# Attention groups reordered to B, C, A with paired scores and half-bank turns, and the in-projection's weight subtractions moved from DVE to GpSimd

## The chip, the core and the metric

The kernel runs on one core of a Trainium2 chip. The metric is the device time of one execution in microseconds. TensorE (PE) multiplies matrices from SBUF into PSUM, which has four double banks here (`ps[0]` to `ps[3]`, each 128 partitions by 1024 float32, that is two banks of 512). DVE (VectorE) and ACT (ScalarE) read PSUM and SBUF, POOL (GpSimd) reads SBUF only, SP issues most DMAs.

## The reference

Two layers over 1024 tokens of width 1024, all float32. In each layer a normed input goes through one projection of 2820 columns, which three groups of heads share, each with its own attention. Their outputs are concatenated (1024 wide), projected and added; then comes an MLP of width 4096.

```python
h = rmsnorm(x, g_mix[l]);  proj = h @ w_in[l]
aq, ak, av, bq, bk, bv, cq, ck, cv, cf = jnp.split(proj, offsets, axis=-1)
# A: 4 heads x 2 maps of dim 64, chunk-causal, alibi:  a = softmax(s0) - lam * softmax(s1);  o = rmsnorm(a @ v) * (1 - lam_init), v is 128 wide
# B: 4 query heads on 2 key heads, keys of the last 128 tokens (two blocks), alibi, a sink in the softmax's sum
# C: 4 heads, causal, forget gate:  s + cum[q] - cum[k],  cum = cumsum(log_sigmoid(cf + c_fbias))
x = x + jnp.concatenate([o_a, o_b, o_c], axis=-1) @ w_out[l]
x = x + jnp.square(jax.nn.relu(rmsnorm(x, g_mlp[l]) @ w_up[l])) @ w_down[l]
# after both layers: rmsnorm(x, g_final)
```

## The kernel before

**Precision.** Every product of float32 operands is made of three fp32r matmuls: high by high, high by low, low by high. The high part is a rounding copy by ACT, the low part a subtraction by DVE. This holds for weights, activations, queries, keys, values and probabilities.

**Dense work.** All matrices are kept transposed, features in partitions, tokens along the free side. A slab is 128 output columns of a weight matrix: 1024x128, loaded into `w_raw` by two DMAs, split into `w_hi` and `w_lo` (two slots). A slab's product with the activations is eight chunks of 128 contraction rows; one chunk is six matmuls of 512 columns (`piece`, L1192 to L1199, and `products`, L1136 to L1151). A layer has 23 slabs of in-projection, 8 of out-projection and 64 of MLP.

**Attention.** Eight pairs of maps per layer: four of A (a head's two maps), two of C and two of B (two heads each). For each pair there are eight blocks of 128 queries; block i sees i+1 blocks of keys (in B at most two). In A and B one step is one query block with both maps, in C one step is one query block of one head, so a C pair has sixteen steps. PE makes scores in `ps[0]` (L1259 to L1269), DVE adds the bias and takes the row maximum (`biased_max`, L933), ACT exponentiates (L629). For A, DVE combines both maps (`combine`, L952). PE transposes the probabilities block by block into `ps[2]` (`turn_probs`, L1271), ACT and DVE split them into `pt_hi` and `pt_lo` (L597 and L922, four blocks at a time), PE multiplies by the values into `ps[3]` (`values`, L1283), DVE adds the two halves of the result (`sum_values`).

**Scores.** In A and C the scores of one map fill up to both banks of `ps[0]`, so a map's scores wait until DVE has read those of the map before. A map's operands lie in 64 partitions (0 to 63 or 64 to 127). In B a map needs one bank, and the two maps' scores are issued one behind the other, in different banks.

**Order.** It is written out by hand and every engine walks the same list of steps (`Run`, L105). In step t PE issues: scores of t, a chunk of the in-projection, values of t-2, scores of t's second map (A), another chunk, transposes of t-1, the remaining chunks (L1346 to L1380). The in-projection's chunks are spread over the steps by `PIECES` and `END_PIECES` (L99 and L100): a pair's steps carry the three slabs of the next pair. The order is A (a loop over two pairs, twice), C, then C, B, B. Only the first four slabs are computed ahead of attention. The last slab is done near the start of B: the last pair of B carries no chunk.

**Around it.** C's bias is cum[q] - cum[k] plus the causal mask, written to `probs` by ACT (L594) and DVE (L1003). The attention outputs of all heads are transposed after the last step (`turn_out`, L1391) and split by ACT and DVE; then the out-projection runs. The layer's input `xt` (4 MB) is saved to DRAM by one DMA on SP's queue once `h` is complete (L395), in front of the load of slab 2, and comes back in two DMAs. DVE computes `w_lo` for all slabs (L809, L841); POOL only adds squares and scales A's outputs.

## Time and profile before

| | us |
|---|---|
| median of 3 runs (lowest, highest) | 2849.33 (2838.36, 2854.39) |
| the profiled execution's own time | 2837.89 |
| its span, first to last instruction | 2835.8 |
| TensorE busy | 2723.2 (96%) |
| DVE busy | 1226.4 (43%) |
| ACT busy | 958.7 (34%) |
| POOL busy | 92.5 (3%) |
| mean granted TensorE clock | 0.965 |

A busy share is taken over the whole span. Matmuls overlap in the records, since they are pipelined: the distance between two starts is what a matmul costs, not the duration of one. The granted clock is in parts of 2.4 GHz: 1.0 is 2.4 GHz and 0.5 is 1.2 GHz, and a value in between is a mixture over the stretch.

### The profile page before, as it was taken

What the parts mean: (1) busy time and instruction counts of PE and PEld (TensorE: products, weight loads), DVE (VectorE), ACT (ScalarE), POOL (GpSimd) and SP (SyncE); (2) the same over time, 40 slices, a digit from 0 to 9 for tenths busy, and PEclk for the clock granted to TensorE, in tenths of its full rate; (3) what the DMA queues carried; (4) which work ended last, traced back from release to release, by engine and by line L of the source; (5) the groups of instructions that cost most, each with busy time, mean ns of one, the idle gap of its engine ahead of it and who ended that gap; (6) DMA issues with size and microseconds to landing.
All of it is one profiled execution on the core that took longest, in us unless ns stands there. A gap on an engine that the chain in (4) does not pass through costs nothing.

```text
span 2835.8 us, 35362 instructions
## 1 busy us (share of the span) xinstructions
PE 2723.2 (96%) x12809; PEld 2211.0 (78%) x12809; DVE 1226.4 (43%) x2444; ACT 958.7 (34%) x1700; POOL 92.5 (3%) x51
## 2 busy tenths in 40 slices
PE   7999999979999999999999999998899999999998
PEld 6777777768888888888877777776788888888887
DVE  5565665654322322223436666656443223232334
ACT  4444454552321212112234444545423122130223
POOL 0000010001000000000200001000020000000001
PEclk9999999959999999999999999998899999999998
DMA  4100000012111111111130000000211111111112
GB/s 153 38 23 23 22 23 16 8 38 82 45 52 45 47 50 49 47 50 46 44 104 23 23 22 23 16 23 8 82 52 45 45 51 48 48 44 52 44 52 74
DMA packets 214389, 126.25 MB, mean 45 GB/s; under 512 B 14702, under 2 KB 213400, under 8 KB 213528
## 3 DMA queue, kind: packets, MB, share of 16 engines
q1 hardware_dynamic: 211176, 121.95, 14.4%
q10 hardware_dynamic: 3120, 3.15, 0.3%
q8 instruction: 48, 0.79, 0.1%
q14 instruction: 45, 0.37, 0.0%
HBM read 112.49 MB, written 12.58 MB: 44 GB/s over the span
## 4 chain that ended last, share of the span: by engine, by line
PE 84%; DVE 6%; ACT 4%; issue 3%; DVEq 1%; DMA 1%; SPq 0%; ACTq 0%; POOL 0%; POOLq 0%
PE ps L1149 54%; PE ps L1196 17%; PE ps L1266 5%; PE ps L1296 2%; PE ps L1278 1%; ACT probs L632 1%; PE ps L1298 1%; DVE probs L940 1%; PE ps L1155 1%; DVEq L943 1%; DVE part L856 1%; PE ps L1408 1%; PE ps L1218 1%; DVE neg_max L948 1%; DVE part L853 1%
## 5 line engine op out<-in xcount | busy, mean ns | idle before, releaser
L1149 PE MATMUL ps<-h_hi,w_hi 128*128 128x512 f32 x1024 | 315.6, 389 | 0.0
L1060 DVE TENSOR_TENSOR xt<-ps,xt 128x1024 f32 (+1 forms) x80 | 98.0, 1225 | 503.1 <-PE ps L1149 501.6
L1149 PE MATMUL ps<-h_lo,w_hi 128*128 128x512 f32 x1024 | 315.3, 389 | 0.0
L1149 PE MATMUL ps<-u_hi,w_hi 128*128 128x512 f32 x1024 | 315.2, 389 | 0.0
L1149 PE MATMUL ps<-u_lo,w_hi 128*128 128x512 f32 x1024 | 315.2, 389 | 0.0
L1149 PE MATMUL ps<-h_hi,w_lo 128*128 128x512 f32 x1024 | 315.2, 389 | 0.0
L1149 PE MATMUL ps<-u_hi,w_lo 128*128 128x512 f32 x1024 | 315.2, 389 | 0.0
L477 ACT ACTIVATE w_hi<-w_raw 128x1024 fp32r<-128x1024 f32 x144 | 151.2, 1050 | 454.8 <-PE ps L1149 436.5
L1196 PE MATMUL ps<-h_hi,w_hi 128*128 128x512 f32 x736 | 265.5, 443 | 34.4 <-DVE v_parts L845 12.7
L1196 PE MATMUL ps<-h_lo,w_hi 128*128 128x512 f32 x736 | 237.4, 405 | 0.0
L1196 PE MATMUL ps<-h_hi,w_lo 128*128 128x512 f32 x736 | 235.0, 401 | 0.0
L720 ACT ACTIVATE ring<-ring 128x1024 f32<-128x1024 f32 x64 | 67.8, 1060 | 487.1 <-DVE ring L1080 487.1
L1149 PEld LDWEIGHTS ps<-h_lo,w_hi 128*128 128x128 f32 x1024 | 192.2, 188 | 40.0
L1149 PEld LDWEIGHTS ps<-h_hi,w_lo 128*128 128x128 f32 x1024 | 192.2, 188 | 40.0
L1149 PEld LDWEIGHTS ps<-u_lo,w_hi 128*128 128x128 f32 x1024 | 192.2, 188 | 39.9
L1149 PEld LDWEIGHTS ps<-u_hi,w_hi 128*128 128x128 f32 x1024 | 192.2, 188 | 39.9
L1149 PEld LDWEIGHTS ps<-u_hi,w_lo 128*128 128x128 f32 x1024 | 192.2, 188 | 39.9
L1149 PEld LDWEIGHTS ps<-h_hi,w_hi 128*128 128x128 f32 x1024 | 191.9, 188 | 39.6
L1080 DVE SCALAR_TENSOR_TENSOR ring<-ps,inv_rms 128x1024 f32<-128x1024 f32 x64 | 78.4, 1225 | 322.9 <-PE ps L1149 311.0
L1296 PE MATMUL ps<-v_parts,pt_hi 128*128 128x128 f32 (+1 forms) x696 | 182.0, 327 | 24.6 <-DVE pt_lo L929 18.6
L632 ACT ACTIVATE probs<-probs,neg_max,slope_now 128x256 f32<-128x256 f32 (+7 forms) x128 | 111.2, 868 | 255.7 <-DVE neg_max L946 255.5
L1196 PEld LDWEIGHTS ps<-h_hi,w_hi 128*128 128x128 f32 x736 | 120.9, 195 | 87.4 <-issue 57.3
(159 smaller groups left out, 4000.3 us busy)
## 6 DMA issues: line engine op xcount, KB each, us to landing
w_raw<-in_w_up_dram SPq DMA_DIRECT2D x128, 256.0 KB, 3.1
w_raw<-in_w_down_dram SPq DMA_DIRECT2D x128, 256.0 KB, 3.0
w_raw<-in_w_in_dram SPq DMA_DIRECT2D x92, 256.0 KB, 3.3
x_saved<-xt SPq DMA_DIRECT2D x2, 4096.0 KB, 11.9
w_raw<-in_w_out_dram SPq DMA_DIRECT2D x32, 256.0 KB, 3.0
xt<-x_saved SPq DMA_DIRECT2D x4, 2048.0 KB, 7.4
out_dram<-rows SPq DMA_DIRECT2D x4, 1024.0 KB, 5.6
rows<-in_x_dram ACTq DMA_DIRECT2D x3, 1024.0 KB, 14.0
```

Source lines behind the costliest of these rows:

```text
L477: nc.scalar.activation(w_hi[:, j], w_raw[:], ACT.Copy).then_inc(w_hi_done, 1)
L632: e = nc.scalar.activation(probs[:, n % 4, 0:width], probs[:, n % 4, 0:width], ACT.Exp, bias=neg_max[:, n % 8:n % 8 + 1], scale=sl, accum_ ...
L720: nc.scalar.activation(ring[j][:], ring[j][:], ACT.Square)
L853: e = V.scalar_tensor_tensor(out=part[:], in0=ps[p][:], scalar=q_scale[:, bass.ds(pair, 1)], in1=inv_rms[:], op0=ALU.mult, op1=ALU.mult)
L856: e = V.tensor_tensor(part[:], ps[p][:], inv_rms[:], ALU.mult)
L940: V.tensor_tensor_reduce(out=probs[:, n % 4, 0:width], in0=ps[0][:, p0:p0 + width], in1=bias, scale=1.0, scalar=-3e38, op0=ALU.add, op1=AL ...
L1060: V.tensor_tensor(xt[:, 2 * m + j], r, xt[:, 2 * m + j], ALU.add).then_inc(evacuated, 1)
L1080: V.scalar_tensor_tensor(out=ring[j][:], in0=r, scalar=0.0, in1=inv_rms[:], op0=ALU.max, op1=ALU.mult).then_inc(evacuated, 1)
L1149: mm = nc.tensor.matmul(ps[j][:, bass.ts(t, BANK)], w[:, j, c], h[:, c, bass.ts(t, BANK)], start=(c == 0 and n == 0), stop=(c == NC - 1 an ...
L1196: mm = nc.tensor.matmul(ps[p][:, bass.ts(t, BANK)], w[:, j, c], h[:, c, bass.ts(t, BANK)], start=(c == 0 and n == 0), stop=(c == NC - 1 an ...
L1266: mm = nc.tensor.matmul(ps[0][:, p0 + at:p0 + at + w], q[half, qs, i * P:(i + 1) * P], k[half, ks, k0 * P + at:k0 * P + at + w], start=(p ...
L1296: nc.tensor.matmul(o.rearrange("p (h e) -> p h e", h=2), pt_hi[:, b0 + k * blocks + b], v_parts[:, slot, k0 + b, :, e0:e1], start=(b == 0) ...
```

## The change

The order of the pairs is B, B, C, C, A, A, A, A, written out without a loop. Both maps of a pair are scored together: `scores(t, ph)` takes keys of up to 512 positions (phase 0, and phase 1 where there are more than four blocks), map 0 in one bank of `ps[0]` and map 1 in the other, and alternates between the maps for each of the three products. C has steps of both heads, like the others. Its bias drops cum[q], which is constant along a row of the softmax, and its causal mask is added by a matmul of the identity with the mask.

Transposed probabilities are handled in halves of at most four blocks, one bank of `ps[2]` each, the two banks in turn. Each half is a slot of its own in the order; a step has as many slots as the step before has halves (one, two, or in C up to four). A slot of PE is: scores phase 0 (the step's first slot), half of the slot's chunks, the transposes of one half of step t-1, the values of the half transposed in the slot before, scores phase 1, the remaining chunks. Values of half h wait for the split of h, transposes for that of h-2.

The heads' outputs are transposed in slots too (`MIX_AT`), and in the last pair's slots PE computes the first six chunks of three slabs of the out-projection; their last two chunks are added afterwards from a small extra load. POOL instead of DVE makes `w_lo` for the in-projection's slabs from the third on. `xt` is saved by eight DMAs on ACT's queue, chunk by chunk, and comes back in eight. SBUF is laid out in two regions that change roles between the layers. A's heads are normed from sums in SBUF. The MLP's loops compute the same in nearly the same order.

The diff cut to its core (removed lines only where they are short):

```diff
-    PIECES = {"A": [4, 4, 3, 3, 2, 3, 3, 2], "C": [1] * 4 + [2] * 6 + [1, 2, 1, 2, 1, 1], "B": [2] + [1] * 6 + [0]}
-    END_PIECES = {"A": [4, 4, 3, 3, 2, 2, 2, 2, 2], "C": [2] * 7 + [1] * 9 + [1], "B": [0] * 9}
...
-                sp.dma_start(x_saved, xt[:].rearrange("p c s -> p (c s)")).then_inc(x_spilled, 16)
...
+    ORDER = [("B", 0), ("B", 1), ("C", 0), ("C", 1), ("A", 0), ("A", 1), ("A", 2), ("A", 3)]
...
+    FILL = [[4, 5], [6, 7]] + [[8 + 3 * n, 9 + 3 * n, 10 + 3 * n] for n in range(5)]
...
+    LATE = 6
+    NPARTIAL = 3
...
+    PIECES = {0: [2] * 8, 1: [2] * 8, 2: [0, 3, 4, 4, 4, 4, 3, 2], 3: [0, 3, 4, 4, 4, 4, 3, 2]}
+    for p in range(FIRST_A, PAIRS - 1):
+        PIECES[p] = [0, 4, 4, 4, 3, 3, 3, 3]
+    PIECES[PAIRS - 1] = [0, 1, 3, 4, 4, 3, 3, 0]
+    MIX_AT = {56: [0, 1], 57: [2, 3], 58: [4, 5], 62: [6]}
+    SCALE_AT = {FIRST_A * NQ + 2 * NQ + 3: (0, 2), FIRST_A * NQ + 3 * NQ + 3: (2, 3)}
...
+    for t in range(NT + 1):
+        mine = []
+        if t:
+            grp, b = ORDER[(t - 1) // NQ][0], window(t - 1)[1]
+            if grp == "A":
+                mine = [add_half(t - 1, [(0, at, min(4, b - at))]) for at in range(0, b, 4)]
+            elif 2 * b <= 4:
+                mine = [add_half(t - 1, [(0, 0, b), (1, 0, b)])]
+            else:
+                mine = [add_half(t - 1, [(j, at, min(4, b - at))]) for j in range(2) for at in range(0, b, 4)]
+            mine[-1].last = True
+        for slab in MIX_AT.get(t, []):
+            mine += [add_half(None, [(0, 4 * side, 4)], slab, side) for side in range(2)]
...
+                def restore(c):
+                    sp.wait_ge(turned, NHALF * l + mix_ready[c])
+                    sp.dma_start(xt[:, c], x_saved[:, c]).then_inc(x_back[c], 16)
...
+                for n in range(2, IN):
+                    pool.wait_ge(w_hi_done, LOADS * l + n + 1)
+                    j = w_slot(l, n)
+                    nc.gpsimd.tensor_tensor(w_lo[:, j], w_raw[:], w_hi[:, j].bitcast(F32), ALU.subtract).then_inc(w_split, 1)
+                for n in range(AH - 1):
+                    pool.wait_ge(o_inv_done, 3 * l + (1 if n < 2 else 2))
+                    o = o_out[:, FIRST_A + n].rearrange("p (b e) -> p b e", e=P)
                     nc.gpsimd.tensor_tensor(o, o, o_inv[:, n * NQ:(n + 1) * NQ].unsqueeze(2).to_broadcast([P, NQ, P]),
...
+            def spill(c):
+                act.dma_start(x_saved[:, c], xt[:, c]).then_inc(x_spilled, 16)
...
+                def half_high(half):
+                    act.wait_ge(turned, NHALF * l + half.index + 1)
+                    bank = bank_of(l, half)
...
+                def biased_max(t, ph):
+                    p, i = t // NQ, t % NQ
+                    grp, n = ORDER[p]
+                    k0, blocks = window(t)
+                    key0, key1 = BANK * ph, min(blocks * P, BANK * (ph + 1))
+                    width = blocks * P
+                    dve.wait_ge(scored, NPHASE * l + PHASE0[t] + ph + 1)
+                    before = [h.index + 1 for h in halves if h.step is not None and h.step <= t - 2]
+                    if before:
+                        dve.wait_ge(turned, NHALF * l + before[-1])
+                    V.memset(wait_slot[:], 0.0)
+                    to = far_max if ph else row_max
+                    a = (2 * t) % 8
+                    for j in range(2):
+                        if grp == "A":
+                            bias = far[:, S - width + key0:S - width + key1]
+                        elif grp == "B":
+                            bias = near[:, 2 * P - width:2 * P]
+                        else:
+                            bias = o_out[:, FIRST_A + 2 * n + j, key0:key1]
+                        e = V.tensor_tensor_reduce(out=probs[:, (2 * t + j) % 4, key0:key1],
+                                                   in0=ps[0][:, BANK * j:BANK * j + key1 - key0], in1=bias, scale=1.0,
+                                                   scalar=-3e38, op0=ALU.add, op1=ALU.max,
+                                                   accum_out=to[:, a + j:a + j + 1])
+                    e.then_inc(scores_read, 1)
...
+                for s in slots:
+                    t = s.step
+                    if s.first and t:
+                        if ORDER[(t - 1) // NQ][0] == "A":
+                            combine(t - 1)
+                    if s.first and t < NT:
+                        biased_max(t, 0)
+                    if s.half:
+                        half_low(s.half)
+                    if s.first and t < NT and phases(t) == 2:
+                        biased_max(t, 1)
+                    if s.first and t and ORDER[(t - 1) // NQ][0] != "A":
+                        invert_sums(t - 1)
+                    if s.summed is not None:
...
+                def scores(t, ph):
+                    p, i = t // NQ, t % NQ
+                    grp = ORDER[p][0]
+                    k0, blocks = window(t)
+                    key0, key1 = BANK * ph, min(blocks * P, BANK * (ph + 1))
+                    if i == 0 and ph == 0:
+                        pe.wait_ge(split_done, NSPLIT * l + max(slab_of(p, Q), slab_of(p, K)))
+                    if NPHASE * l + PHASE0[t] + ph:
+                        pe.wait_ge(scores_read, NPHASE * l + PHASE0[t] + ph)
+                    masked = grp == "C" and key1 == blocks * P
+                    for n, (q, k) in enumerate(((q_hi, k_hi), (q_hi, k_lo), (q_lo, k_hi))):
+                        for j in range(2):
+                            half = slice(j * HD, (j + 1) * HD)
+                            mm = T.matmul(ps[0][:, BANK * j:BANK * j + key1 - key0], q[half, q_slot(p), i * P:(i + 1) * P],
+                                          k[half, kv_slot(p), k0 * P + key0:k0 * P + key1],
+                                          start=(n == 0), stop=(n == 2 and not masked))
+                    if masked:
+                        for j in range(2):
+                            mm = T.matmul(ps[0][:, BANK * j + key1 - key0 - P:BANK * j + key1 - key0], ident_r[:], causal[:],
+                                          start=False, stop=True)
                     mm.then_inc(scored, 1)
 
+                def dense(pieces):
+                    for s, c in pieces:
...
+                def turn_half(half):
+                    if NHALF * l + half.index > 1:
+                        pe.wait_ge(pt_split, NHALF * l + half.index - 1)
+                    bank = bank_of(l, half)
+                    if half.slab is not None:
+                        if half.slab < FIRST_A:
+                            pe.wait_ge(o_normed, NQ * FIRST_A * l + NQ * (half.slab + 1 if half.slab >= 2 else 2))
+                        else:
+                            pe.wait_ge(o_scaled, AH * l + half.slab - FIRST_A + 1)
+                        src = o_out[:, half.slab]
+                    elif ORDER[half.step // NQ][0] == "A":
+                        pe.wait_ge(combined, NQ * AH * l + half.step - NQ * FIRST_A + 1)
...
+                def values(half):
+                    t = half.step
+                    p, i = t // NQ, t % NQ
+                    grp = ORDER[p][0]
+                    k0, blocks = window(t)
+                    pe.wait_ge(pt_split, NHALF * l + half.index + 1)
...
+                for s in slots:
+                    t = s.step
+                    early = (len(s.pieces) + 1) // 2
+                    if s.first and t < NT:
+                        scores(t, 0)
+                    dense(s.pieces[:early])
+                    if s.half:
+                        turn_half(s.half)
+                    if s.values:
+                        values(s.values)
+                    if s.turns_v is not None:
+                        pe.wait_ge(evacuated, EVACS * l + slab_of(s.turns_v, V_) + 1)
+                        turn(part, ps[1], NQ, v_turned)
+                    if s.first and t < NT and phases(t) == 2:
+                        scores(t, 1)
+                    dense(s.pieces[early:])
+
...
+                pe.wait_ge(scores_read, NPHASE * (l + 1))
+                pe.wait_ge(w_split, LOADS * l + OUT + 4)
+                out_piece(3, 0, 0, True, False)
+                out_piece(3, 1, 0, False, False)
+                values(slots[-1].half)
+                for slab in range(2, NC - 1):
+                    if slab == LATE:
+                        pe.wait_ge(pt_split, NHALF * l + mix_ready[LATE])
+                    out_piece(3, slab, 0, False, False)
+                for half in MIX_LAST:
+                    turn_half(half)
```

## Rows read from the trace of the kernel before

**Rows 1.** The page, its first two parts: busy time of TensorE, then the granted clock by slices.
```profile
PE 2723.2 (96%) x12809; PEld 2211.0 (78%) x12809; DVE 1226.4 (43%) x2444; ACT 958.7 (34%) x1700; POOL 92.5 (3%) x51
PEclk9999999959999999999999999998899999999998
```

**Rows 2.** Busy time by stage, the second layer: stretch, its length, engines, clock, DMA.
```profile
1422.00:1477.00 55.00, 53.47 (x251) 42.63 (x251) 21.14 (x17) 19.30 (x20) 2.33 (x1) 0.99 0.39 131
1477.00:1759.00 282.00, 268.66 (x1329) 209.59 (x1330) 176.54 (x468) 127.16 (x301) 0.00 (x0) 0.98 0.08 22
1759.00:1846.00 87.00, 82.70 (x446) 64.55 (x446) 52.52 (x148) 48.09 (x99) 7.56 (x4) 0.97 0.09 21
1846.00:1931.00 85.00, 82.63 (x435) 65.50 (x436) 47.89 (x151) 43.15 (x96) 0.00 (x0) 0.93 0.07 17
1931.00:2008.00 77.00, 60.63 (x329) 49.28 (x328) 44.25 (x188) 44.57 (x139) 0.00 (x0) 0.69 0.03 8
2008.00:2108.00 100.00, 97.64 (x452) 80.79 (x452) 44.43 (x31) 31.86 (x32) 16.34 (x7) 0.98 0.25 83
2108.00:2808.00 700.00, 700.00 (x3106) 580.08 (x3104) 207.90 (x168) 149.73 (x146) 18.74 (x8) 1.00 0.16 47
```

**Rows 3.** Instructions in order of time, TensorE, one step of group B.
```profile
542.61 0.39 PE L1266 MATMUL ps<-k_hi,q_hi 64*128 64x256 f32 x2
542.84 0.29 PE L1266 MATMUL ps<-k_lo,q_hi 64*128 64x256 f32 x2
543.17 0.33 PE L1296 MATMUL ps<-v_parts,pt_hi 128*128 128x128 f32 x1
...
544.97 0.44 PE L1278 MATMUL ps<-ident,probs 128*128 128x128 f32 x2
```

**Rows 4.** Instructions in order of time, TensorE, one step of group A.
```profile
1603.49 0.49 PE L1266 MATMUL ps<-k_hi,q_hi 64*128 64x512 f32 x1
...
1604.73 0.39 PE L1266 MATMUL ps<-k_hi,q_lo 64*128 64x512 f32 x1
1605.04 0.73 PE L1196 MATMUL ps<-h_hi,w_hi 128*128 128x512 f32 x2
...
1606.53 0.93 PE L1278 MATMUL ps<-ident,probs 128*128 128x128 f32 x7
```

**Rows 5.** Groups of instructions by line and shape, DVE and ACT.
```profile
L940 DVE CUSTOM_DVE_ANT_0 probs<-ps,far 128x512 f32<-128x512 f32 x16 | 11.0, 689 | 2.0 <-issue 2.0
L940 DVE CUSTOM_DVE_ANT_0 probs<-ps,near 128x256 f32<-128x256 f32 x56 | 23.7, 423 | 5.0 <-issue 5.0
L948 DVE TENSOR_SCALAR neg_max<-row_max,sink,neg_slope 128x1 f32<-128x1 f32 x64 | 17.5, 273 | 6.5 <-issue 0.4
L956 DVE RECIPROCAL inv_sum<-row_sum 128x2 f32<-128x2 f32 x64 | 9.9, 155 | 0.0
L961 DVE SCALAR_TENSOR_TENSOR probs<-probs,lam_ratio 128x1024 f32<-128x1024 f32 x8 | 10.3, 1286 | 0.6
L604 ACT ACTIVATE pt_hi<-ps 128x384 fp32r<-128x384 f32 x32 | 15.5, 485 | 0.0
L632 ACT ACTIVATE probs<-probs,neg_max,slope_now 128x1024 f32<-128x1024 f32 x16 | 19.9, 1242 | 33.6 <-DVE neg_max L946 33.6
L632 ACT ACTIVATE probs<-probs,neg_max,slope 128x256 f32<-128x256 f32 x64 | 38.4, 600 | 65.5 <-DVE neg_max L948 48.1 <-DVE neg_max L946 13.7
L632 ACT ACTIVATION_READ_ACCUMULATOR probs<-probs,neg_max,slope_now 128x1 f32 x128 | 23.8, 186 | 0.0
```

**Rows 6.** Groups of instructions by line and shape, GpSimd and DVE.
```profile
L453 POOL TENSOR_TENSOR sq_sum<-sq_sum,ring 128x1024 f32<-128x1024 f32 x28 | 67.3, 2405 | 238.8 <-ACT ring L482 230.3 <-ACT ring L764 8.5
L1068 DVE SCALAR_TENSOR_TENSOR h_lo<-xt,param,h_hi x16 | 36.7, 2295 | 39.6 <-ACT h_hi L483 39.6
L819 DVE SCALAR_TENSOR_TENSOR h_lo<-xt,param,h_hi 128x1024 fp32r<-128x1024 f32 x9 | 12.7, 1411 | 1.1 <-ACT h_hi L483 1.0
```

**Rows 7.** The chain that ended last, first layer: start, length, what.
```profile
38.21 12.76 DMA w_raw<-in_w_in_dram
```

1525 lines of the change are left out of this document (727 added, 798 removed).

## The prediction

> **What bounds the kernel.** I read the page's first two parts first. TensorE is busy for 2723 of 2836 us, DVE for less than half [rows 1]: the time is TensorE's list of work, and a gain must shorten that list or its 4% of gaps and slow clock. The clock line dips in two places, and both are inside attention. So next the busy time by stage, for the second layer, which has no start-up in it [rows 2]. Its stages are: first four slabs 55 us, the four A pairs 282 (70.5 each), the first C pair 87 (with the bias maps between the C pairs), the second C pair 85, B 77, the out-projection 100, the MLP 700. The MLP is 64 slabs of 8 chunks at full clock without a gap: 1.367 us a chunk, and the diff leaves it so. B stands out: PE busy for 61 of 77 us and a mean clock of 0.69, so for about 62% of it the array ran at 1.2 GHz. Its last pair has no chunks to fill waits with. What the change can move is the 686 us before the MLP, in each layer.
>
> **Unit costs.** A chunk inside attention: 1.367 plus 0.13 for the switch to and from short matmuls, so 1.5. (Estimate: the A stage has 96 chunks, and 0.13 makes its sum come out.) Transposes: 7 in 0.93 us, 0.13 each [rows 4]. Values: eight blocks from 543.17 to 544.97, 0.225 each [rows 3]. Scores of one map with 1024 keys: 1603.49 to 1605.04, 1.55 us for six matmuls, of which 6 x 0.227 is streaming and about 0.2 is start and switch [rows 4]; with the entry I take 0.27 a call.
>
> **Paired scores.** In B both maps' scores are already issued back to back, in different banks and partition halves. The trace shows "k_hi,q_hi x2" within 0.39 us and all six 256-column matmuls in 543.17 - 542.61 = 0.56 us [rows 3]. One behind the other they would need 6 x 107 = 640 ns for the columns alone. So the two halves of the array work at the same time, and a pair of matmuls costs what one does. The change brings this to A and C. For one such pair of maps (36 blocks each): before 2 x 3 x 4608 columns at 2.4 GHz = 11.5, gaps 1.0, 16 calls x 0.27 = 4.3, together 16.8 us; after 5.8 + 0.5 + 12 calls x 0.27 = 9.5. That is 7.3 us less for each of six pairs, 44 a layer. C's mask adds 2 x 16 matmuls of 128 columns at 0.11 to 0.13: 4 us. Bounds: nothing, if 512 columns do not overlap as 256 do (then 4 us are lost), and 48.
> The Trainium skill (TensorEngine Tiling (Array Packing), Key Properties) says that a change of tiling mode drains TensorE, which speaks against many short score calls. The trace has a trace of it: from the last score matmul to the next chunk are 1605.04 - 1604.73 = 0.31 us instead of 0.23 [rows 4]. It is in the 0.27 a call above, and the calls become fewer.
>
> **B first, with chunks.** The 16 steps carry 32 chunks instead of 8. A step: scores 0.56 + 0.1, transposes 4 x 0.13 = 0.5, values 4 x 0.225 = 0.9, two chunks 3.0, together 5.1; sixteen are 81 us. Its chain (two maxima of 256 at 0.423 and two small operations each 0.273, 1.9 with hand-offs; two exponentials at 0.6 + 0.186 and the two of the sinks, about 2.3 [rows 5]; ACT's copy of the last half before them) is about 5 us from the end of scores, and PE has 6.6 us of work in that time, so it is hidden. The 24 chunks more would have cost 36 us elsewhere, so B's own part falls from 65 us to 33: this is the second large gain.
>
> **C.** 24 chunks 36, scores 9.5 + 2, transposes 72 x 0.13 = 9.4, values 72 x 0.225 = 16.2, turning V 1: 74 us. Transposes wait for one exponential only, which is a slot or more back; I add 4 for waits. Twice 78 = 156, against 172 with the bias maps.
>
> **A, where the gain is given back.** Work: chunks 36, scores 9.5, transposes 4.7, values 8.1, V 1: 59 us. Before, PE had a whole step of work between a map's scores and the transposes that need them. Now scores phase 1 come late in a step and the combined map is wanted early in the next. Take the step with 8 blocks, from the moment T at which the combined map of the step before is ready. Transposes to T+0.5. DVE's two 512-wide maxima take 2 x 0.689 + 0.15 = 1.5 and free `ps[0]` at T+1.7 [rows 5]. Scores phase 1 then end at T+2.7. PE goes on: two chunks to 5.7, three transposes and their latency to 6.2. ACT copies that half (0.485) until 6.7, and only then exponentiates both maps: 2 x (1.242 + 0.186) = 2.86, to 9.6 [rows 5]. DVE: reciprocal, ratio and combination of 1024, 0.7 + 1.29, to 11.6. (The wait for maxima, phase 1, ends earlier: 2.9 + 1.5 + 2 x 0.273 + 0.2 = 5.2.) PE's work in these 11.6 us: 0.5 + 0.45 + 0.95 + 3.0 + 0.4, then values 0.9, the next pair's scores and no chunk (`PIECES` starts with 0): 7.2 us. So 4.4 us of waiting. The step before, by the same sum: 10.9 - 8.3 = 2.6. The two before that about 1.2 each. Together 9.4 us a pair: 59 + 9.4 + 0.6 for V = 69 us against 70.5 now. Three pairs are 207. Bounds: no wait (59) to 3 us more in four steps (81).
> The last pair has 18 chunks of the out-projection (27), scores, transposes, values and V 23.3, and 56 transposes of outputs 7.3: 57.6. It has no chunk in its last step and none behind it, where the chain is bare: waits 15. That makes 73.
>
> **Tail, head.** After the last step 46 chunks remain: 63 us, and 4 for the chain through the norm of the last head, which five chunks cover almost wholly. Before, this stage took 100 us with 64 chunks and 64 transposes. The head gets two bias maps more: 58.
>
> **GpSimd's subtractions.** POOL's 128x1024 tensor_tensor takes 2.405 us [rows 6]. A slab takes PE 12 us and more, and its low half is wanted a slab later: hidden. It takes work off DVE, which is not the bound: worth nothing in itself. While POOL works, DVE's two-input operation on SBUF slows from 1411 to 2295 ns [rows 6]. POOL is busy for 21 x 2.4 = 50 of about 480 us, so a tenth of the combinations lies under it: 3 us a layer.
> The Trainium skill (GPSIMD Engine Reference, Key points) says that GpSimd shares its SBUF interfaces with VectorE, with contention where a DVE instruction has two SBUF inputs. The trace agrees (the 2295 ns). Were all 32 combinations of a layer under it, that would be 28 us, still on the faster side.
>
> **Sum.** A layer before its MLP: 58 + 81 + 156 + 207 + 73 + 67 = 642; plus 3 for GpSimd and 5 for table loads of A's square roots inside the chain and hand-offs: 650, against 686. Two layers: -72. The first layer has one thing more: slab 2's load sits behind the 4 MB save of `xt` and is waited for, 12.76 us in the chain [rows 7]. The save now goes out in eight parts on ACT's queue as the chunks are made, and the load is no longer queued behind it. I take -10: the whole wait less some 3 us for ACT, which issues eight DMAs between its copies. Bounds: 0 and -13. So 2837.9 - 82 = 2756 for the profiled execution. The median of the runs lies 11 us above that execution; I forecast 2760.
>
> **Rivals.** All sums are for the profiled time.
> (a) Forecast: 2715 to 2800, chance 0.55.
> (b) The waits in A are half as long, for ACT's copies and DVE's maxima run ahead of my chain, and the clock stays up: A 5 less a pair, last pair 7 less, C 3 less each, twice: 2700. For: before, waits in this stage are only 13 of 282 us. Against: there the chain had a step more. 0.20.
> (c) The chain is longer: each hand-off between engines costs 0.1 more, twelve a step, four steps a pair, five us a pair: 2756 + 2 x 4 x 5 = 2796, up to 2834 with step 0 of each pair worse. 0.13.
> (d) Slower: TensorE's clock falls in the A pairs. In B it fell with PE at work about half of the time; in A's last four steps it would be at work 70%. Half of those 34 us at 1.2 GHz adds 17 us a pair: 2756 + 8 x 17 = 2892. It decides from about 10 us a pair. 0.08.
> (e) Pairing does nothing at 512 columns, because two weights must then be loaded per 227 ns: 2756 + 2 x 44 = 2844, no change. Against: in B six loads pass in 0.56 us, 0.19 a pair [rows 3]. 0.04.
>
> **How the numbers follow.** 2760 is (a). The range 2685 to 2825 takes in (a), most of (b) and (c). A difference under 0.5% (14 us) can't be told from none here. Faster by more: (a), (b) and (c), 0.88. Within: (e) and the edge, 0.05. Slower: most of (d), 0.07.
>
> **What would show it.** Score matmuls in A and C come in twos that start together, and one such two follows the other at 0.23 us. The mean clock in B is over 0.95. B takes about 81 us, a C pair 78, an A pair 69, the stage after it 67. PE's waits in A name the combined map on DVE, longest at a pair's start and before the last values. No DMA wait over 3 us near 38 us. It is wrong if A pairs take under 62 or over 76 us, or if the clock in A falls under 0.9.

## The result, and the profile after

| | before | after |
|---|---|---|
| median of 4 runs (lowest, highest) | 2846.38 (2838.36, 2854.39) | 2873.95 (2870.01, 2878.04) |
| ratio, 95% interval | 1 | 1.0097 [1.0061, 1.0133] |
| profiled span | 2835.8 | 2876.2 |
| mean granted clock of TensorE | 0.965 | 0.952 |

The change makes the kernel slower by 1.0%. I had forecast 2760 us, 3% faster.

First the head of the page (columns as in [rows 1]).

```profile
PE 2674.1 (93%) x12857; PEld 2175.5 (76%) x12857; DVE 1164.2 (40%) x2367; ACT 897.7 (31%) x1580; POOL 192.8 (7%) x91
PEclk9998899988999999999999989997899999999999
```

TensorE is busy for 49 us less, as a shorter list of work should make it, but the span is 40 us longer: its gaps grew from 2835.8 - 2723.2 = 113 us to 2876.2 - 2674.1 = 202. The busy time fell by less than the list, too. The granted clock has only the levels 1.0 and 0.5 here, so a mean of 0.952 stands for 9.6% of the span at 1.2 GHz, 276 us, and 0.965 before for 198. By this estimate, which takes TensorE as busy in all of the 78 us more at 1.2 GHz, half speed adds up to 39 us to the busy time. The deep dip of the clock in B (5 in [rows 1]) is gone. There are shallow ones instead, in more slices.

The second layer by stage, after (columns as in [rows 2]): head, B, C, A's first three pairs, the last pair up to its last step's scores, from there to the MLP, MLP.

```profile
1436.00:1496.80 60.80, 58.37 (x249) 43.60 (x248) 19.12 (x14) 21.11 (x22) 12.77 (x5) 0.95 0.19 51
1496.80:1575.60 78.80, 76.03 (x450) 59.91 (x450) 46.83 (x177) 49.09 (x144) 7.16 (x3) 0.97 0.08 22
1575.60:1748.30 172.70, 154.99 (x879) 126.94 (x878) 75.57 (x230) 67.52 (x152) 14.48 (x6) 0.90 0.07 19
1748.30:1972.90 224.60, 193.00 (x1024) 151.61 (x1022) 126.81 (x370) 85.86 (x201) 23.84 (x10) 0.92 0.08 22
1972.90:2057.00 84.10, 63.21 (x323) 49.94 (x322) 47.12 (x122) 34.96 (x75) 1.90 (x1) 0.84 0.19 55
2057.00:2145.20 88.20, 78.57 (x348) 64.79 (x348) 46.48 (x53) 30.37 (x41) 16.35 (x7) 0.90 0.17 48
2145.20:2845.00 699.80, 697.54 (x3087) 577.82 (x3086) 199.94 (x161) 141.25 (x138) 18.68 (x8) 1.00 0.16 47
```

| stage | forecast | measured | difference |
|---|---|---|---|
| head | 58 | 60.8 | +3 |
| B | 81 | 78.8 | -2 |
| C, two pairs | 156 | 172.7 | +17 |
| A, three pairs | 207 | 224.6 | +18 |
| last pair and tail | 140 | 172.3 | +32 |
| GpSimd, tables | 8 | in the stages | -8 |
| layer before its MLP | 650 | 709.2 | +59 |

The busy times in the rows say of what kind the excess is. In C I had 148 us of work and 8 of waits: measured are 155.0 busy and 17.7 idle. In A's three pairs I had 179 and 28: measured are 193.0 and 31.6. So in A most of the 18 us is matmuls that take longer, at a mean clock of 0.92, and only a small part is more idle time.

Before, this layer took 686 us, so it is 23 us longer; the first layer's attention is 13 us longer, and the rest is the MLPs and the end. B came out as worked out. Everything behind it did not.

Who TensorE waited for, over both layers (engine, tile and line, us in total, times, longest), first before, then after:

```profile
PE ps L1296 <- DVE pt_lo L929: 18.6, 24, 2.3
PE ps L1196 <- DVE v_parts L845: 12.7, 12, 1.9
PE ps L1196 <- DVE part L853: 9.7, 12, 0.9
```

```profile
PE ps L1264 <- DVE probs L920: 73.0, 36, 5.9
PE ps L1116 <- DVE part L804: 31.9, 12, 3.0
PE ps L1116 <- DVE part L801: 15.3, 14, 2.0
```

L920 is the combination of A's two maps: the wait I had expected to be the largest. L804 and L801 are the evacuations of a finished slab from `ps[1]`, for which the next slab's first chunk (L1116) waits. These 47 us were not in my sum.

What such a wait drags along is seen in one A step (i = 5, 15.1 us; its neighbours take 7.0 and 7.9). Instructions in order of time (start, length, what; in brackets the idle time before it and what ended it):

```profile
1868.31 0.46 DVE L904 TENSOR_SCALAR neg_max<-row_max,far_max,neg_slope 128x1 f32<-128x1 f32 x2
...
1869.01 1.22 DVE L804 TENSOR_TENSOR part<-ps,inv_rms 128x1024 f32<-128x1024 f32 x1
...
1870.37 1.19 PE L1116 MATMUL ps<-wide_hi,w_hi 128*128 128x512 f32 x2 [2.98 <-DVE part L804]
1871.36 1.05 PE L1116 MATMUL ps<-wide_lo,w_hi 128*128 128x512 f32 x2
1872.21 1.05 PE L1116 MATMUL ps<-wide_hi,w_lo 128*128 128x512 f32 x2
...
1873.07 0.41 PE L1264 MATMUL ps<-ident,probs 128*128 128x128 f32 x1
...
1873.52 0.28 ACT L631 ACTIVATE pt_hi<-ps 128x128 fp32r<-128x128 f32 x1 [3.99 <-PE ps L1264]
1873.69 1.05 ACT L576 ACTIVATE k_hi<-part 128x1024 fp32r<-128x1024 f32 x1
...
1874.64 1.02 ACT L613 ACTIVATE probs<-probs,neg_max,slope 128x768 f32<-128x768 f32 x1
```

A slab ended in the slot before, and its evacuation is DVE's last work of that slot, behind the maxima of scores phase 1. The next slot of TensorE begins with the next slab's first chunk: it waits 2.98 us, and the transposes stand behind it in TensorE's queue, though their probabilities are ready. ACT, whose exponentials follow the copy of these transposes, is idle for 3.99 us, then also copies the finished slab (1.05), and starts the exponentials at 1874.64, when the row maxima had been there since 1868.77. The combined map, and with it the next step's transposes, come that much later. The chunk behind the wait is slow as well: its pairs start 0.99 and 0.85 us apart, where a pair in a long dense stretch takes 0.45 (the last two rows of this section). The granted clock (the value behind the busy times) is 0.50 in this stretch, that is 1.2 GHz. It was 1.00 from 1862.0 to 1867.4, and TensorE did nothing from 1867.4 to 1870.4:

```profile
1870.30:1873.10 2.80, 2.73 (x7) 2.08 (x8) 0.00 (x0) 0.00 (x0) 0.00 (x0) 0.50 0.00 0
```

So one wait costs in three places: TensorE stands, the exponentials come late, and the matmuls behind it run at half speed.

```profile
2139.63 0.61 PE L1116 MATMUL ps<-wide_hi,w_hi 128*128 128x512 f32 x2
2140.08 0.62 PE L1116 MATMUL ps<-wide_lo,w_hi 128*128 128x512 f32 x2
```

In C and A the steps inside which the running sum of the pair's chunks crosses 8 or 16 are the longest or stand out from their neighbours: in the second layer steps 3 and 5 of C (12.8 and 19.1 us, then 11.3 and 16.3) and step 5 of A (12.3, 15.1, 15.5). `PIECES` for A is 0, 4, 4, 4, 3, ...: 8 is reached at a step's end, 16 is not. They aren't the only long ones: step 0, which has no chunks, takes 9.2 to 13.0 us in A's three pairs and in C's second.

### The profile page after: what moved, and what is told of

Same layout as the page of the kernel before. It is cut to its first block, busy times and chain, and to the rows that moved or that the text cites. A ratio compares the mean times of both kernels' runs of the same rounds, so it can differ in the third digit from the quotient of the medians.

```text
span 2876.2 us, 34048 instructions
## 1 busy us (share of the span) xinstructions
PE 2674.1 (93%) x12857; PEld 2175.5 (76%) x12857; DVE 1164.2 (40%) x2367; ACT 897.7 (31%) x1580; POOL 192.8 (7%) x91
## 3 DMA queue, kind: packets, MB, share of 16 engines
q8 instruction: 62, 1.02, 0.2%
## 4 chain that ended last, share of the span: by engine, by line
PE 84%; DVE 7%; ACT 5%; issue 3%; DMA 1%; DVEq 0%; SPq 0%; ACTq 0%; POOL 0%; POOLq 0%
PE ps L1116 72%; PE ps L1264 3%; PE ps L1211 3%; PE ps L1284 2%; ACT probs L613 2%; PE ps L1286 1%; DVE probs L920 1%; ACT pt_hi L631 1%; PE ps L1097 1%; DVE part L804 1%; PE ps L1161 1%; DVE part L801 1%; DVE probs L888 1%; DVE pt_lo L943 1%; DVE wide_lo L938 0%
## 5 line engine op out<-in xcount | busy, mean ns | idle before, releaser
L1116 PE MATMUL ps<-wide_hi,w_hi 128*128 128x512 f32 x3016 | 976.8, 406 | 66.2 <-DVE part L804 31.9
L1116 PE MATMUL ps<-wide_lo,w_hi 128*128 128x512 f32 x3016 | 947.9, 396 | 0.0
L1116 PE MATMUL ps<-wide_hi,w_lo 128*128 128x512 f32 x3016 | 944.8, 395 | 0.0
L1116 PEld LDWEIGHTS ps<-wide_hi,w_hi 128*128 128x128 f32 x3016 | 555.5, 192 | 203.8 <-issue 90.0
L1116 PEld LDWEIGHTS ps<-wide_lo,w_hi 128*128 128x128 f32 x3016 | 578.7, 192 | 125.9
L1116 PEld LDWEIGHTS ps<-wide_hi,w_lo 128*128 128x128 f32 x3016 | 576.1, 191 | 124.3
L613 ACT ACTIVATE probs<-probs,neg_max,slope 128x256 f32<-128x256 f32 (+7 forms) x256 | 201.3, 788 | 14.2 <-DVE neg_max L904 10.3
L1264 PEld LDWEIGHTS ps<-ident,probs 128*128 128x128 f32 x696 | 95.1, 157 | 105.2 <-issue 86.6
L1284 PEld LDWEIGHTS ps<-v_parts,pt_hi 128*128 128x128 f32 x696 | 150.5, 216 | 30.0 <-DVE pt_lo L943 27.6
L1286 PE MATMUL ps<-v_parts,pt_lo 128*128 128x64 f32 (+1 forms) x696 | 170.8, 253 | 0.0
L498 POOL TENSOR_TENSOR w_lo<-w_raw,w_hi 128x1024 fp32r<-128x1024 f32 x42 | 104.2, 2481 | 903.2 <-ACT w_hi L520 903.2
L1286 PEld LDWEIGHTS ps<-v_parts,pt_lo 128*128 128x128 f32 x696 | 150.9, 217 | 0.1
L1047 DVE TENSOR_TENSOR w_lo<-w_raw,w_hi 128x1024 fp32r<-128x1024 f32 x112 | 136.4, 1218 | 0.4 <-ACT w_hi L687 0.4
## 6 DMA issues: line engine op xcount, KB each, us to landing
first_rows<-in_x_dram ACTq DMA_DIRECT2D x3, 1024.0 KB, 13.3
```

The source lines that it names most:

```text
L498: nc.gpsimd.tensor_tensor(w_lo[:, j], w_raw[:], w_hi[:, j].bitcast(F32), ALU.subtract).then_inc(w_split, 1)
L613: e = A.activation(probs[:, (2 * t + j) % 4, 0:width], probs[:, (2 * t + j) % 4, 0:width], ACT.Exp, bias=neg_max[:, at:at + 1], scale=sl, ...
L1047: V.tensor_tensor(w_lo[:, z], w_raw[:], w_hi[:, z].bitcast(F32), ALU.subtract).then_inc(w_split, 1)
L1116: mm = T.matmul(ps[p][:, bass.ts(t, BANK)], w, h[:, bass.ts(t, BANK)], start=(start and n == 0), stop=(stop and n == 2))
L1264: tr = T.transpose(ps[2][:, at:at + P], src[:, b * P:(b + 1) * P], ident[:])
L1284: T.matmul(o.rearrange("p (h e) -> p h e", h=2), pt_hi[:, bank, at], v_parts[:, kv_slot(p), k0 + b, :, e], start=(b == 0), stop=False)
```

## The experiments

Ratios are to the kernel before, with 95% interval; the difference to the changed kernel (1.0097) is in us of 2846. Lengths of single steps and stages are of the second layer of one profiled execution. Experiments 1 to 6 edit the changed kernel, 7 to 11 go on from experiment 2, 12 edits the kernel before.

**1. DVE subtracts again.**

```diff
-                for n in range(2, IN):   # GpSimd
-                    nc.gpsimd.tensor_tensor(w_lo[:, j], w_raw[:], w_hi[:, j].bitcast(F32), ALU.subtract).then_inc(w_split, 1)
+                split_load(l, n)         # DVE, at its place in each slot, as before
```

> The changed kernel with one part undone: DVE computes the in-projection's low halves again. Theory P (GpSimd's subtraction costs time, by slowing DVE or by being late): 5 to 15 us faster than the changed kernel (ratio to before 1.005 to 1.008 instead of 1.010). Theory N (that part is neutral): DVE gets 42 x 1.2 = 50 us more in its order, of which some lies in front of things that PE waits for: 0 to 10 us slower than the changed kernel (ratio 1.010 to 1.013).

Measured: 2891.35 us, 1.0158 [1.0122, 1.0194]: 17 us slower than the changed kernel, more than either theory had. The intervals overlap, but the fastest run here (2886.85) is slower than the slowest of the changed kernel (2878.04). The subtraction on GpSimd is a gain, where I had priced it at a loss of 3 us a layer. Besides DVE's 42 times 1.22 us of work there is its place in line: in this kernel DVE waits in order for ACT's high half, and ACT makes that behind its exponentials. Waits of DVE on this, first experiment 1, then the changed kernel:

```profile
DVE w_lo L765 <- ACT w_hi L516: 94.4, 54, 3.1
```

```profile
DVE w_lo L769 <- ACT w_hi L520: 46.0, 21, 3.1
```

In the changed kernel 48 us of DVE standing still are gone, and the combined maps are waited for 73.0 us instead of 81.1. How the 17 us divide between the work and the standing in line, no run here separates.

**2. Slabs end with a step.** The same 24 chunks a pair, placed so that 8 and 16 are reached at the end of a step.

```diff
-    ... 2: [0, 3, 4, 4, 4, 4, 3, 2], 3: [0, 3, 4, 4, 4, 4, 3, 2]}
+    ... 2: [0, 4, 4, 4, 4, 3, 3, 2], 3: [0, 4, 4, 4, 4, 3, 3, 2]}
-        PIECES[p] = [0, 4, 4, 4, 3, 3, 3, 3]
+        PIECES[p] = [0, 4, 4, 4, 4, 2, 3, 3]
```

> The changed kernel with other chunk counts for C and A (PIECES 0,4,4,4,4,3,3,2 and 0,4,4,4,4,2,3,3), so that a slab of the in-projection ends with a step of the list and not inside one. Theory S (the lost time is where a slab ends inside a step: the next slab's first chunk waits for DVE to empty ps[1], and PE stands in front of its other work): the steps of 12.8 and 16 to 19 us in C and of 15 us in A fall to the length of their neighbours, 5 us in each of 7 places a layer: 50 to 70 us faster than the changed kernel, faster than before too (ratio 0.985 to 0.993). Theory W (the lost time is the wait for the combined map): the long steps shrink but others grow, under 15 us (ratio over 1.004).

Measured: 2824.71 us, 0.9927 [0.9899, 0.9955]: 48 us faster than the changed kernel, and faster than before. The same waits:

```profile
PE ps L1264 <- DVE probs L920: 76.1, 35, 5.9
...
PE ps L1116 <- DVE part L801: 8.0, 14, 0.9
PE ps L1116 <- DVE part L804: 7.0, 12, 0.9
```

The waits for evacuation fell from 47.2 to 15.0 us, those for the combined map did not fall. Step 5 of A takes 7.4 to 8.8 instead of 12.3 to 15.5 us, with one chunk less; steps 4 and 6 are some 1 to 3 us longer in the first two pairs. The page shows of what the gain is made:

```profile
PE 2647.5 (94%) x12857; PEld 2156.5 (76%) x12857; DVE 1164.1 (41%) x2367; ACT 895.9 (32%) x1580; POOL 191.8 (7%) x91
```

TensorE makes the same 12857 matmuls in 26.6 us less busy time (2674.1 before the edit), and its gaps fell by 26.1 us, from 202.1 to 176.0. The mean clock is 0.963 instead of 0.952. So only half of the gain is waits that are gone; the other half is matmuls that no longer run at half speed.

**3. TensorE kept busy in the wait.**

```diff
+                        if half.units[0][1] == 0:      # first half of an A step
+                            for _ in range(6):
+                                T.matmul(ps[2][...], ident_r[:], wide_hi[here][:, 0, 0:BANK], start=True, stop=True)
```

> The changed kernel with six more matmuls of 512 columns in each step of group A, whose results are overwritten, just ahead of PE's wait for the combined map. Theory K (the waits themselves matter less than the half clock that follows them): the six matmuls (1.4 us) lie inside the wait, the clock in A stays at 1.0, and the kernel is 10 to 30 us faster than the changed one. Theory W (the waits are what costs): no change to 15 us slower, since in the steps without a wait 1.4 us are added (about 16 steps a layer: up to 40 us slower) and the clock gives little back.

Measured: 2907.5 us, 1.0221 [1.0186, 1.0256], 35 us slower, at a clock of 0.964 against 0.952. The six matmuls cost 1.3 us where there was no wait, and only in the steps that begin a pair did they bring something (7.6 instead of 9.2 us). The wait for the combined map fell from 73.0 to 31.5 us, those for evacuation stayed (31.9 and 15.3). The 384 matmuls that the edit adds are some 87 us of work at 0.23 each, and TensorE is busy for only 59 us more, so by this estimate the others got faster by about 28. So the clock gave something back, and the added work cost more than that. This way of raising the clock doesn't pay; it doesn't show that the clock costs nothing.

**4. Both maps in the same partitions,** so that they can't overlap. The second map's scores are then made from the first map's operands, and the result is not the kernel's.

```diff
-                            half = slice(j * HD, (j + 1) * HD)
+                            half = slice(0, HD)
```

> The changed kernel, but both maps of a pair take their operands from partitions 0 to 63 (so the second map's scores are wrong), and the array can't work on both at once. Theory O (pairing works at 512 columns and is worth what was forecast): 34 us of columns more in each layer, of which a part falls into waits: 40 to 65 us slower than the changed kernel (ratio 1.024 to 1.033). Rival (pairing doesn't overlap at 512 columns, or lies in waits anyway): within 10 us of the changed kernel.

Measured: 2931.24 us, 1.0319 [1.0277, 1.0361]: the pairing is worth 2931 - 2874, about 57 us by these medians (63 by the ratios). The score matmuls of one call, in pairs, first this kernel, then the changed one:

```profile
1764.78 0.72 PE L1211 MATMUL ps<-k_hi,q_hi 64*128 64x512 f32 x2
1765.35 0.63 PE L1211 MATMUL ps<-k_lo,q_hi 64*128 64x512 f32 x2
1765.82 0.62 PE L1211 MATMUL ps<-k_hi,q_lo 64*128 64x512 f32 x2
```

```profile
1862.00 0.50 PE L1211 MATMUL ps<-k_hi,q_hi 64*128 64x512 f32 x2
1862.34 0.40 PE L1211 MATMUL ps<-k_lo,q_hi 64*128 64x512 f32 x2
1862.57 0.40 PE L1211 MATMUL ps<-k_hi,q_lo 64*128 64x512 f32 x2
```

0.47 us from pair to pair against 0.23. The edit also takes the overlap from B, which had it before the change: B takes 82.9 and 83.0 us in the two layers instead of 79.0 and 78.8. So about 8 of the 57 to 63 us are B's, and the pairing that is new, in C and A, is worth some 49 to 55. I had 88 us of raw work for both layers. The wait for the combined map is 55.1 us here instead of 73.0, so some of the work falls into waits.

**5. All chunks of a slot late where a slab begins** (counts of the changed kernel).

```diff
-                    early = (len(s.pieces) + 1) // 2
+                    early = 0 if s.pieces and s.pieces[0][1] == 0 else (len(s.pieces) + 1) // 2
```

> The changed kernel with its own chunk counts; only, where a slab's first chunk stands in a slot, PE issues all of the slot's chunks behind the slot's transposes and values instead of half of them ahead. Theory S (a slab that ends inside a step costs, since PE stands before the next slab's first chunk until DVE has emptied ps[1], and the transposes and both exponentials stand behind it): PE has 1 to 2 us of other work first and the exponentials no longer wait: 25 to 50 us faster than the changed kernel (ratio 0.993 to 1.001), most of what aligned slabs gave. Rival (the aligned counts helped because more chunks stand in the right steps, not because of the slab's end): within 12 us of the changed kernel (ratio over 1.006).

Measured: 2878.52 us, 1.0123 [1.01, 1.0145], no gain (7 us above the changed kernel, with intervals that overlap). The waits for evacuation fell to 17.7 + 3.3 us, the C pairs got shorter (77.3 and 86.5 us instead of 83.1 and 89.7), but those for the combined map rose from 73.0 to 100.6. In A's steps 1 and 3 a slab begins with the step, and there the two early chunks had stood ahead of the wait for the combined map: in the second and third pair these steps grew from 8 to 13.3 and 10.6 us. The edit did two things at once.

**6. The same only inside a step.**

```diff
-                    early = (len(s.pieces) + 1) // 2
+                    early = 0 if s.pieces and s.pieces[0][1] == 0 and not s.first else (len(s.pieces) + 1) // 2
```

> The counts of chunks per step are those of the changed kernel. Only where a slab's first chunk falls inside a step (not into its first slot), all chunks of that slot are issued behind the transposes and values of the slot, so that TensorE does something else while VectorE empties the bank. Theory (the inside end of a slab is what costs, because TensorE stands before the next slab's first chunk with transposes and exponentials behind it): the waits on the in-projection's evacuations (31.9 us in 12 and 15.3 us in 14 in the changed kernel) fall by half or more, the long C and A steps (19.1, 16.3, 12.3, 15.1 us) get shorter, the steps in which a slab begins at the step's start stay as they are, and the kernel is 15 to 35 us faster than the changed one: ratio 0.998 to 1.004. Rival (only the number of chunks in the steps matters, so that the gain of the aligned counts came from their more even load): within 8 us of the changed kernel, ratio 1.007 to 1.013.

Measured: 2836.41 us, 0.9984 [0.9968, 1.0]: 32 us faster than the changed kernel by ratio, with its counts of chunks. So two thirds of experiment 2's gain come from the order in TensorE's queue alone, without moving a chunk. Waits for evacuation 20.4 + 10.4, for the combined map 69.7, mean clock 0.957. The other third (16 us) isn't separated. Half of the waits for evacuation are still there (30.8 us, 15.0 in experiment 2), and step 5 of A still takes 12.5 to 14.4 us; but experiment 2 also moves a chunk from step 5 to an earlier step, and that can be part of it.

**7. Experiment 2, and the small extra load split later.** In the last pair ACT splits an extra load of the out-projection ahead of the exponentials of step 62. In the changed kernel:

```profile
2043.24 0.84 ACT L514 ACTIVATE xw_hi<-w_raw 128x768 fp32r<-128x768 f32 x1 [4.43 <-DMA w_raw<-in_w_out_dram]
2044.11 0.96 DVE L764 TENSOR_TENSOR xw_lo<-w_raw,xw_hi 128x768 fp32r<-128x768 f32 x1 [4.05 <-ACT xw_hi L514]
2044.14 1.01 ACT L613 ACTIVATE probs<-probs,neg_max,slope 128x768 f32<-128x768 f32 x1
...
2048.05 1.08 PE L1264 MATMUL ps<-ident,probs 128*128 128x128 f32 x4 [5.92 <-DVE probs L920]
```

ACT waits 4.43 us for the DMA with the exponentials behind it, and TensorE then waits 5.92 us for the combined map.

```diff
-            if e + 2 == EXTRA - 1:
-                s.split.append(EXTRA)
+    [s for s in slots if s.step == NT - 1][-1].split.append(EXTRA)
```

> The aligned kernel with the split of the small extra load of the out-projection moved from the slot behind the second partial slab to the end of step 63, behind that step's exponentials. Theory D (in the last pair ACT stands 4.4 us before that load, with the exponentials behind it, and PE waits 5.9 us for the combined map): 4 to 6 us less a layer, and some clock: 8 to 14 us faster than the aligned kernel (ratio 0.988 to 0.990). Rival (the wait moves to the load of the next slab at the end): within 4 us.

Measured: 2806.07 us, 0.9878 [0.9853, 0.9903], 14 us under experiment 2 by ratio. Step 62 takes 10.6 us instead of 17.8, and 10.6 instead of 17.3 in the first layer: these are the 14 us. With experiment 11, which can't be told from it, this is the fastest kernel that computes the whole, 1.2% faster than before. Its second layer from C to the MLP:

```profile
1541.50:1699.40 157.90, 146.09 (x881) 118.88 (x880) 76.00 (x230) 66.87 (x152) 14.27 (x6) 0.96 0.08 21
1699.40:1910.10 210.70, 185.26 (x1021) 146.43 (x1020) 126.18 (x370) 85.49 (x201) 23.50 (x10) 0.95 0.09 23
1910.10:1986.10 76.00, 58.99 (x329) 46.15 (x327) 46.13 (x122) 34.49 (x75) 1.90 (x1) 0.91 0.21 61
1986.10:2073.30 87.20, 75.97 (x344) 63.07 (x344) 47.36 (x55) 30.54 (x41) 16.32 (x7) 0.90 0.17 49
```

The edit touches only the last pair. That C and A's three pairs take 157.9 and 210.7 us here and 160.8 and 214.8 in experiment 2 shows how far such stages vary without a reason in the list.

**8. Experiment 2 with the combination over 64 columns.** The rest of the combination is left out, so the result is not the kernel's.

```diff
-  V.scalar_tensor_tensor(out=probs[:, (2 * t) % 4, 0:width], in0=probs[:, (2 * t + 1) % 4, 0:width], ...
+  V.scalar_tensor_tensor(out=probs[:, (2 * t) % 4, 0:HD], in0=probs[:, (2 * t + 1) % 4, 0:HD], ...
```

> The aligned kernel, but A's two maps are combined in 64 columns only (the rest of the combination is left out), 0.25 us instead of 0.35 to 1.29. Theory W (in A PE waits for exponentials and combination in the steps with 7 and 8 blocks, in the pair's first and the last pair's bare steps): the cut comes out of PE's time in about half of the steps: 0.9 us x 16 a layer, 20 to 35 us faster than the aligned kernel. Rival (something else binds there): under 8 us.

Measured: 2798.9 us, 0.9847 [0.9827, 0.9868], 23 us under experiment 2 by ratio, from 34 us of DVE work. The waits for the combined map are 51.4 instead of 76.1. So the combination's own length is part of A's waits. What the 51.4 us that are left consist of isn't shown.

**9. Experiment 2 with the outputs' transposes spread.**

```diff
-    MIX_AT = {56: [0, 1], 57: [2, 3], 58: [4, 5], 62: [6]}
+    MIX_AT = {54: [0], 55: [1, 2], 56: [3], 57: [4], 58: [5], 62: [6]}
```

> The aligned kernel with the transposes of the heads' outputs spread over steps 54 to 58 (slabs 0; 1, 2; 3; 4; 5) instead of 56 to 58 (two each). Theory M (step 56 takes 18 us because six halves go one by one through ACT and DVE with little work for PE beside them): step 56 falls to 13 and the two steps before it grow by less than 2, since they carry chunks: 4 to 7 us a layer, 8 to 14 us faster than the aligned kernel (ratio 0.988 to 0.990). Rival (the halves cost the same wherever they stand, as more slots lengthen the chain of the steps with 7 and 8 blocks): within 4 us or slower.

Measured: 2824.36 us, 0.9933 [0.9912, 0.9955], no difference to experiment 2. Step 56 went from 17.7 to 11.1 us, step 55 from 10.0 to 17.7: each is the step that holds six halves, two of its own and four of outputs, and it takes 17.7 us at either place.

**10. Experiment 7 with exponentials first.** In A's steps with two halves ACT does both exponentials ahead of the half's copy (the branch for the other steps is left out here).

```diff
+                    ahead = not s.first and FIRST_A * NQ < s.step < NT
+                    if ahead:
+                        for j in s.exps:
+                            exponentials(s.step, j)
```

> Aligned counts and late load as in the fastest kernel so far (2806 us), and in those A steps that hold two halves in a slot ScalarE does both exponentials before the copies of the halves, not each behind its half's copy. Theory (the chain of scores, exponentials, probabilities and combined map sets the length of A's steps): the chain is about 1.5 us shorter in three to four steps of each A pair, four pairs, two layers, less what the copies then cost: 15 to 35 us faster, ratio 0.976 to 0.983. Rival (the copies are wanted just as early by the values matmuls): their wait takes the place of the one removed, within 6 us of 2806, ratio 0.986 to 0.990.

Measured: 2817.93 us, 0.992 [0.9902, 0.9939]: 12 us slower than experiment 7, where the theory had 15 to 35 us faster and the rival no more than 6 either way. Waits for the combined map 69.5 before and 71.1 now. Steps 6 and 7 of A's first pair take 13.6 + 8.4 us where they took 12.0 + 10.0, step 1 9.3 instead of 7.3. That the copies are needed at least as early as the exponentials would explain it, but isn't shown: in the first layer A's three pairs take 214.6 us in both kernels. Part of the difference lies in C's second pair (85.5 instead of 82.6 us), which the edit doesn't touch: its first step takes either 10.6 or about 13 us in these kernels, and I don't know why.

**11. Experiment 7 with six idle matmuls,** as in 3, but only in query blocks 6 and 7.

```diff
+                        if half.units[0][1] == 0 and half.step % NQ >= NQ - 2:
```

> As the kernel of 2806 us, with six extra matmuls over 512 columns (their result isn't used) ahead of the wait for the combined map in query blocks 6 and 7 only, where the waits are longest. If TensorE's half clock behind the waits is a cost of its own: granted clock up, the matmuls behind the wait at full speed, 5 to 15 us faster (ratio 0.983 to 0.986). Rival (the wait is the chain's and ends when it ends; the matmuls only fill it): no change or up to 5 us slower, ratio 0.987 to 0.990.

Measured: 2804.62 us, 0.9869 [0.9847, 0.9891]: the same as experiment 7 (0.9878). Clock 0.970 against 0.967. The first steps of the second and third pair fell from 9.2 and 10.4 to 7.6 us, as in experiment 3, but steps 6 of these pairs grew from 10.5 to 11.6 and 12.0.

**12. The kernel before with GpSimd's part alone.**

```diff
+                for s in range(2, SPLIT):   # GpSimd
+                    pool.wait_ge(w_hi_done, NSLAB * l + s + 1)
+                    nc.gpsimd.tensor_tensor(w_lo[:, s % 2], w_raw[:], w_hi[:, s % 2].bitcast(F32), ALU.subtract).then_inc(w_split, 1)
```

> The kernel before with one part of the change alone: GpSimd instead of DVE subtracts the low halves of the in-projection's slabs from the third on (21 a layer). In the changed kernel the same part was worth 17 us (undone: 1.0158 against 1.0097). Theory (DVE is late because it stands behind ScalarE's high half of the weights, whatever the order of the heads): the kernel before gains too, 8 to 18 us, ratio 0.994 to 0.997. Rival (the part pays only where the chain through DVE sets a step's length, which the paired scores brought about): within 5 us of the kernel before, ratio 0.998 to 1.002; were GpSimd's longer subtraction (2.48 us instead of 1.22) on the path of the next slab's first chunk, slower, 1.002 to 1.006.

Measured: 2828.16 us, 0.9961 [0.9947, 0.9975]: 11 us faster than before, at a clock of 0.969 against 0.965. So the part pays under either order of the heads. TensorE waits for GpSimd's subtraction once, 6.84 us until 54.5 us, where the kernel before waits 6.96 us until 54.7, both behind the load of [rows 7]; that the longer subtraction comes too late was not seen. The gain isn't in TensorE's direct waits, which hardly moved (19.2 and 13.1 us for the two longest, before 18.6 and 12.7): of the 13.7 us by which the profiled span is shorter, 11.0 are busy time (2712.2 instead of 2723.2), at the higher clock.

## Why the prediction was wrong

**The failed step** is the one that gave C and A their waits: "I add 4 for waits" for C and "9.4 us a pair" for A. I worked out the chain of one step between scores and the combined map and took a chunk to cost 1.5 us wherever it stands. I didn't ask whether the first chunk of a slab may start. The list let slabs end inside a step, with the evacuation last in DVE's slot and the next slab's first chunk first in TensorE's. The wait for it, 47.2 us over both layers, had no term in my sum, and neither had the half speed of the matmuls behind it: the chunk above takes 2.7 us instead of 1.5. Experiment 2 ends slabs with steps, at the price of moving one chunk a pair, and 48 us are gone. Experiment 6 gets 32 of them by the place in the queue alone. In experiments 2 and 7 C takes 160.8 and 157.9 us for my 156, A's three pairs 214.8 and 210.7 for my 207. So the sums of C and A nearly come out once these waits are gone. That my chain was right step by step isn't shown by this: experiment 10, which was forecast from it, went the other way.

One unit cost was misread and hid a part of this. I took 0.13 us for a transpose, from the 0.93 us of seven in [rows 4]; but that holds the pipeline's end of the last one, and the next chunk starts 0.68 us after the first:

```profile
1607.21 0.71 PE L1196 MATMUL ps<-h_hi,w_hi 128*128 128x512 f32 x2
```

That is 0.10 each. For the 144 transposes of C the forecast was some 4 to 5 us too high, and for A's three pairs some 3 to 4.

**The last pair and the tail** (73 and 67 forecast, 172.3 together): experiment 7 takes out the wait for the extra load, and 163.2 stay. 87.2 of these lie behind the last step's first scores, in two parts:

```profile
1986.10:1996.00 9.90, 6.11 (x28) 4.32 (x27) 8.46 (x21) 3.65 (x8) 0.00 (x0) 0.67 0.18 53
1996.00:2006.00 10.00, 4.35 (x21) 4.38 (x22) 4.16 (x7) 4.29 (x9) 0.00 (x0) 0.50 0.18 55
```

In the first 20 us TensorE is busy for 10.5, at a falling clock, with two waits for the combined map of 3.7 and 5.7 us. The 67.3 us behind them are the chunks, as forecast (67). So the 23 us that are missing lie in the last pair with its last step, 96 us for my 73. Step 56 at 17.7 us is one cause (the outputs' transposes, experiment 9: not to be had back by moving them). I had counted their 7.3 us of work and not their 14 halves that pass through `ps[2]` with ACT and DVE behind. My 15 us for the bare chain were too little as well: TensorE is idle for 26 of the 96 us. No experiment divides the 23 us between these. Twice 23 is the distance between experiment 7 (2806) and my 2760, so this part of the miss stays open.

**Paired scores**: forecast 2 x 44 less 2 x 4 for the mask = 80. Experiment 4, which keeps the mask, shows 57 to 63 for C, A and B, so some 49 to 55 for C and A where I had 88: mis-sized. Rival (e), that 512 columns don't overlap, is refuted: pairs start 0.23 us apart. Here the Trainium skill (TensorE: Matmul & The Clock Gate, Part 3) says that matmuls on different row groups run at the same time; the 0.47 and 0.23 us of experiment 4 agree.

**B first**: forecast 81, measured 78.8, clock 0.97. Right; the 2 us are about what the misread transposes (some 60) make.

**GpSimd**: mis-sized and of the wrong sign: 17 us gain in the changed kernel, 11 in the one before. My reason, that DVE "is not the bound", looked at DVE's busy share and not at what stands behind an instruction in its queue; that this is how the gain comes about is likely and not shown apart from the work itself. The contention that I had priced at 6 us exists, but is small for the subtractions. (1411 ns in [rows 6] wasn't a clean base: eight of those nine took 1274 to 1285 ns, the ninth, beside GpSimd, 2485.) Here the combination of 128 columns, with the subtraction on DVE (experiment 1) and on GpSimd:

```profile
L920 DVE SCALAR_TENSOR_TENSOR probs<-probs,lam_ratio 128x128 f32<-128x128 f32 x8 | 2.8, 351 | 0.8 <-issue 0.3
```

```profile
L920 DVE SCALAR_TENSOR_TENSOR probs<-probs,lam_ratio 128x128 f32<-128x128 f32 x8 | 5.1, 639 | 0.6
```

2.3 us in all; the widths from 768 up kept their 1019 to 1285 ns. What I had not seen is another contention that the change brings in. GpSimd's scaling of A's outputs now falls on the combination of 640 columns in the third and the last A pair. First the groups before and after, then one case in order of time:

```profile
L961 DVE SCALAR_TENSOR_TENSOR probs<-probs,lam_ratio 128x640 f32<-128x640 f32 x8 | 7.1, 884 | 1.0 <-issue 0.6
```

```profile
L920 DVE SCALAR_TENSOR_TENSOR probs<-probs,lam_ratio 128x640 f32<-128x640 f32 x8 | 12.7, 1593 | 0.6
```

```profile
1934.59 3.75 POOL L502 TENSOR_TENSOR o_out<-o_out,o_inv 128x1024 f32<-128x1024 f32 x2 [3.61 <-DVE o_inv L974]
1936.61 2.41 DVE L920 SCALAR_TENSOR_TENSOR probs<-probs,lam_ratio 128x640 f32<-128x640 f32 x1
```

Four of the eight took 0.88 us, with no GpSimd operation beside them, and four 2.19 to 2.41. In experiment 1, without GpSimd's subtractions, it is the same (1596 ns in the mean), so it is the scaling. In experiment 2 step 5 takes 8.8 us in the third pair and 7.5 and 7.4 in the first two, so some of this reaches TensorE.

**The clock** (rival (d), the one that came out on the slower side). It did fall: 0.90 in C, 0.92 in A. It fell as a result of waits: with slabs that end with a step it is 0.94 and 0.93 (experiment 2) and 0.96 and 0.95 (experiment 7). But it is a large part of the bill: half of experiment 2's gain is shorter busy time, and the estimate for the changed kernel against the one before was up to 39 us for half speed. Filling the waits with idle matmuls (3, 11) raised the mean clock, but cost as much work or more. I had put (d) at 2892 for the right reason, that waits and slow clock come together. What I had not seen were the waits that set it off.

**The save of `xt`**: the 12.76 us DMA wait of [rows 7] isn't in the chain any more. No gain of 10 came of it: the first attention step starts at 86.6 us, before at 84.4. In the chain the gate's preparation now stands in its place (start, length, what):

```profile
48.45 1.14 ACT gate_tmp L585
...
56.56 4.34 DVE cum L829
```

How much of this the earlier load uncovered, no run here tells.

**The chances**: 0.07 for slower was too little, and 2825 as the upper end had room only for a longer chain, not for a wait that wasn't in the sum. In a list of work that is written anew, such a wait should have been a rival.
